# Moving an SBUF arena by 32 bytes against the activations that stand ahead of it

## What is computed

```python
h = rms_norm(x, attn_norm_g)
proj = h @ w_in                      # q, k, v of two branches, q of the third, 3 gates
m = rms_norm(mem, mem_norm_g)
mk, mv = split(m @ w_mem_kv)
y_a = neighbourhood_attention(qa, ka, va, na_rpb) @ w_branch_a
y_b = dilated_mixture(qb, kb, vb, t5_bias) @ w_branch_b
y_c = memory_attention(qc, mk, mv) @ w_branch_c
merged = gates[0] * y_a + gates[1] * y_b + gates[2] * y_c
x = x + merged @ w_out
h = rms_norm(x, ffn_norm_g)
# router: logits, top 4 of 32, softmax over the four
# expert e: gu = h @ w_gu[e] + b_gu[e]; a = (clip(u) + 1) * (g * sigmoid(1.702 g)); y = a @ w_dn[e] + b_dn[e]
x = x + weighted sum of the experts' y
out = rms_norm(x, final_norm_g)
```

## Time and profile before

| | us |
|---|---|
| median of 3 runs | 1217.89 (1217.21 to 1218.4) |
| the profiled execution, its own time | 1218.3 |
| its span, first to last instruction | 1216.5 |
| TensorE busy in it | 1166.8 |
| HBM read in it | 453.13 MB |

### The profile page before, as it was taken

One profiled execution on the slowest core, in us unless ns is written; L12 is line 12 of the kernel. 1 busy time (PEld: TensorE's weight loads), 2 busy tenths in 40 slices (PEclk: granted clock), 3 DMA queues, 4 the chain that ended last, 5 costly groups with the idle time before them and its releaser, 6 DMA issues.

```text
span 1216.5 us, 14185 instructions
## 1 busy us (share of the span) xinstructions
PE 1166.8 (96%) x6145; PEld 595.8 (49%) x6145; DVE 246.4 (20%) x511; ACT 269.7 (22%) x579; POOL 206.4 (17%) x89
## 2 busy tenths in 40 slices
PE   8999999999999999999999999998999999999996
PEld 7989877898433333333343333333333333333332
DVE  3145132233411121111111211111111111111112
ACT  6457577445210111001010100100000000010002
POOL 5864766785000000000000000000000000000000
PEclk9999999999999999999999999999999999999999
DMA  8775644677999999999999999999999999999994
GB/s 278 262 244 198 212 155 154 226 278 256 424 430 431 430 434 434 415 435 432 431 432 432 430 434 433 433 432 433 433 430 431 431 430 432 430 432 431 431 431 207
DMA packets 62136, 455.15 MB, mean 374 GB/s; under 512 B 5129, under 2 KB 33705, under 8 KB 43512
## 3 DMA queue, kind: packets, MB, share of 16 engines
q1 hardware_dynamic: 62072, 454.22, 90.3%
HBM read 453.13 MB, written 1.07 MB: 373 GB/s over the span
## 4 chain that ended last, share of the span: by engine, by line
PE 65%; DMA 30%; ACT 2%; DVE 1%; POOL 1%; issue 1%; DVEq 0%; SPq 0%; ACTq 0%; POOLq 0%
PE ps L591 63%; DMA arena<-in_expert_w_gate_up 27%; DMA arena<-in_expert_w_down 3%; PE ps L904 1%; PE ps L646 1%; PE ps L898 1%; POOL w_lowc L580 0%; DMA arena<-in_mem 0%; POOL w_lowa L580 0%; ACT arena L1106 0%; ACT arena L1096 0%; ACT L1120 0%; ACT w_high L1076 0%; DVE x_normed L1562 0%; PE ps L642 0%
## 5 line engine op out<-in xcount | busy, mean ns | idle before, releaser
L591 PE MATMUL ps<-arena,gathered_T 128*64 128x512 f32 x2034 | 472.8, 613 | 29.2 <-DMA arena<-in_expert_w_gate_up 29.2
L591 PE MATMUL ps<-arena 128*64 128x512 f32 (+6 forms) x1490 | 316.4, 562 | 3.4 <-issue 2.1
L591 PEld LDWEIGHTS ps<-arena,gathered_T 128*64 128x64 f32 x2034 | 144.9, 140 | 296.5 <-issue 269.2
L591 PEld LDWEIGHTS ps<-arena 128*64 128x64 f32 (+3 forms) x1490 | 113.3, 149 | 196.2 <-issue 193.6
L1229 ACT COPY arena<-ps 128x256 f32<-128x256 f32 x32 | 11.9, 372 | 350.5 <-PE ps L898 350.5
L1506 DVE TENSOR_SCALAR arena<-arena 128x128 f32<-128x128 f32 x64 | 19.3, 344 | 307.2 <-PE ps L898 307.2
L1512 DVE TENSOR_SCALAR arena<-ps 128x512 f32<-128x512 f32 x32 | 22.1, 692 | 275.6 <-PE ps L591 275.6
L1220 ACT ACTIVATE gathered_T<-ps,g_cols 128x128 f32<-128x128 f32 x128 | 36.6, 368 | 173.4 <-PE ps L591 173.4
L591 PEld LDWEIGHTS ps<-arena,x_normed 128*128 128x128 f32 x512 | 59.5, 191 | 24.8 <-issue 24.3
L591 PE MATMUL ps<-arena,x_normed 128*128 128x128 f32 x512 | 65.4, 281 | 0.2 <-DVE arena L1463 0.2
L1239 ACT COPY arena<-ps 128x512 f32<-128x512 f32 x31 | 18.2, 586 | 172.2 <-PE ps L591 172.2
(11 more groups left out here) (229 smaller groups left out, 897.5 us busy)
## 6 DMA issues: line engine op xcount, KB each, us to landing
arena<-in_expert_w_gate_up SPq DMA_DIRECT2D x53, 4096.0 KB, 37.9
arena<-in_expert_w_down SPq DMA_DIRECT2D x61, 2048.0 KB, 38.2
arena<-in_expert_w_gate_up SPq DMA_DIRECT2D x19, 2048.0 KB, 10.8
arena<-in_w_in SPq DMA_DIRECT2D x29, 1024.0 KB, 5.2
arena<-in_expert_w_down SPq DMA_DIRECT2D x6, 1024.0 KB, 38.6
arena<-in_expert_w_gate_up SPq DMA_DIRECT2D x4, 1024.0 KB, 7.1
arena<-in_w_out SPq DMA_DIRECT2D x4, 1024.0 KB, 5.8
arena<-in_w_mem_kv SPq DMA_DIRECT2D x3, 1024.0 KB, 11.5
```

The source lines that it names most:

```text
L591: return nc.tensor.matmul(out, lhsT, rhs, start=start, stop=stop, **kw)
```

## The change

The start of the arena is rounded up to a multiple of 64 as before, and 32 bytes are added: 38944 instead of 38912. Everything that counts from `base` moves with it: ring, weight parts, memory, attention and merged parts, all scratch. Everything made ahead of it stays. No instruction is added, removed or put elsewhere.

```diff
-        base = -(-nc.sbuf_base // 64) * 64
+        base = -(-nc.sbuf_base // 64) * 64 + 32
         MOE0 = RING * CHUNK
         arena = nc.alloc_sbuf_tensor_at("arena", [P, ARENA], F32, offset=base)
```

## The result

| | before | after |
|---|---|---|
| median of 6 runs each, us | 1217.55 (1215.71 to 1218.4) | 1223.88 (1222.14 to 1227.39) |
| ratio | | 1.0056, 95% interval 1.0043 to 1.0069 |
| profiled execution: its own time and its span, us | 1218.3, 1216.5 | 1222.51, 1220.7 |

The changed kernel is slower by 6.3 us by the medians (5.2 to 8.4 by the interval of the ratio, which is worked out from all runs and not from the two medians). The prediction was 1219.2 us with a range up to 1222.5: it fails, and so does its likeliest outcome, no difference that a measurement can tell.

The account below looks back on a forecast made before the run. TensorE bounds the front, before 300 us, and the DMA rate everything behind it. Front terms 1.90 + 0.57 + 0.2 - 1.30 = +1.37 us, taken as +1.3 on the median of 1217.89, gave 1219.2 us; range 1215.5 to 1222.5.

Parts of the forecast that it names:

- TensorE's sum: Front, ahead of 300 us: matmuls whose operands go from different to equal places add +1.37 us of TensorE time.
- A: Front: twelve narrow chunks with h_T_parts moving, 576 matmuls from 116.7 to 120.0 ns, +1.90 us.
- B: Front: seven narrow chunks with h_T_parts stationary, 336 matmuls from 118.3 to 120.0 ns, +0.57 us.
- C: Front: 64 matmuls with late_high moving and merged_T_parts stationary, priced like A, +0.2 us.
- D: Front: ten wide chunks, 240 matmuls from 232.1 to 226.7 ns, -1.30 us.
- The expert stream at no cost: Weight transfers from 304 to 1186 us: no cost taken, bounds 0 and 1.2% of 882 us, 10.6 us.
- the packets' case: Expert stream: packets 32 bytes past a multiple of 64 are slower, 1220.5 to 1229.8 us; chance 0.10.
- third rival: Expert stream: packets 32 past a multiple of 64 take longer into SBUF, up to 1229.8 us; chance 0.10.
- No effect: Front: the 3 and 5 ns differences come from something else, such as PSUM bank or neighbours; 1217.9 us; chance 0.12.
- The place itself: Front: each operand's own place sets matmul pace, not the relation; -5.1 us, 1212.8 us; chance 0.07.
- Expert matmuls, casts and vector work without a cost: Expert matmuls stay at 592 ns; ACT's casts and VectorE's scaling take the same time at either place; 0 us.
- ACT's squares: 1056 ns in the arena, 1105 ns from x_tokens to x_normed; taken as 0, upper bound +0.6 us.

Follow-up runs that it names:

- e2: Only the ring of weight slots 32 bytes higher than in the kernel before, scratch behind it kept at a multiple of 64: 1226.35 us, ratio 1.0070.
- e4: The changed kernel measured again, beside the kernel before: 1224.05 us, ratio 1.0052.
- f4: One chunk per weight transfer from expert 4 on, as in f3, with the arena 32 bytes higher: 1242.96 us, ratio 1.0206 to the kernel before.
- g1: Kernel before with the arena left in place and the activation tensors ahead of it moved down 32 bytes, to multiples of 256: 1218.84 us, ratio 1.0008.
- e3: Kernel before with only the scratch areas behind the ring 32 bytes higher, ring left in place: 1217.41 us, ratio 1.0000.
- f2: Kernel before with the arena 256 bytes higher and 64 floats shorter: 1217.53 us, ratio 0.9993.
- f3: Kernel before with one chunk per weight transfer from expert 4 on (packets of 8192 bytes), arena where it was: 1226.33 us, ratio 1.0068.
- e1: Kernel before with the arena 64 bytes higher and 16 floats shorter: 1223.06 us, ratio 1.0049.
- f1: Kernel before with the arena 128 bytes higher and 32 floats shorter: 1222.37 us, ratio 1.0039.
- g2: Kernel before with the activation tensors moved down to multiples of 256 and the arena 32 bytes higher: 1222.08 us, ratio 1.0037.
- h1: Kernel before with the arena 224 bytes higher and 56 floats shorter: 1221.86 us, ratio 1.0036.
- h2: f3's one-chunk transfers with the arena 224 bytes higher: 1240.52 us, ratio 1.0179 to the kernel before.

## Why the prediction was wrong

**What bounds the kernel: right.** Ahead of 300 us TensorE, behind it the DMA rate alone. It is by this that 0.59% of a rate became 5 us.

**TensorE's sum: right.** Forecast +1.37 us, and by the starts of the matmuls in the two traces: A, 62.85 us instead of 61.32 over eleven of the twelve chunks (the twelfth, in 6, waited for 1.3 us in the trace before), for twelve +1.7 (forecast +1.90); B, 39.92 instead of 39.40, +0.52 (+0.57); C, 7.36 instead of 7.23, +0.13 (+0.2); D, 53.28 instead of 54.39, -1.11 (-1.30). Together +1.2 us. A was over-priced a little because two of its chunks, in 2 and in 3, ran at 117.9 ns before and not at the 116.7 of in 9 that was taken for all. D was over-priced a little because two of its ten chunks, at 76 and 136 us, gained 1.3 to 1.7 ns a matmul and not 5; on the other side the window of the earlier trace rows for in 26 was cut a little short, since the starts of its matmuls stand 233.4 ns apart in the trace before and not 232.1. The whole front, from the first matmul of mem 1 to the last of out, scatters by a microsecond from one execution to the next; in the traces of the five kernels with equal places (the changed one, e2, e4, f4, g1) it took 276.5 to 278.0 us, on average 277.4, in the four with the places of before (before, e3, f2, f3) 275.1 to 276.5, on average 276.1: +1.3 us. TensorE's largest wait between 16 and 298 us went from 2.9 us to 3.4 us. By its letter that is one of the prediction's signs of being wrong, but it is the same wait for ACT and 0.5 us of it, so no new wait took the front's place:

```profile
PE ps L646 <- ACT arena L1106: 3.4, 3, 2.5
```

**The expert stream at no cost: the step that failed.** The prediction took the earlier trace rows, a transfer into x_tokens at 32, as evidence that such packets cost nothing, and gave the packets' case 0.10. The right mechanism was its third rival, but for the boundary, which is 256 bytes and not 64 (e1, f1 and f2), and its bound of 1.2%, 10.6 us, held the measured 0.59% and 5.2 us. Its sign, a stream below 429 GB/s, came by halves: 427 from 400 to 500 us, but 430 from 900 to 1000 us; the long stretch tells it clearly. Two things went wrong in this step.

First, the stretch was too short to show what was asked. 0.6% of 1.5 us is 9 ns, half a packet in eighty, as the text itself could have worked out from its own limit of 0.13%: no row of 1.5 us decides such a question, and the gap of one packet was taken as nothing.

Second, even exact times of its packets would not have shown it. In the changed kernel all packets into the ring start 32 past a multiple of 256, and yet the stretch from 292 to 293.5 us (all packets of 8192 bytes, into the arena) and the stretch of the earlier trace rows, 312.5 to 314 us, read

```profile
DMA packets 77, 0.63 MB, mean 421 GB/s; under 512 B 0, under 2 KB 0, under 8 KB 0
...
q1 hardware_dynamic: 77, 0.63, 99.1%
...
DMA packets 83, 0.64 MB, mean 429 GB/s; under 512 B 3, under 2 KB 3, under 8 KB 5
```

The first gives 0.991 x 16 x 1500 ns / 77 = 308.9 ns a packet, the time of an aligned one; the second 429 GB/s, more than the 426 of the earlier trace rows. In the busy stretch that begins at 300 us the single packets take the old time (309 ns for 8192 bytes) up to about 315 us and some 3 to 10 ns more from there on. The loads of the front behave alike: in one that keeps every DMA engine busy for some 64 packets, the first 50 or so are at the old time and the last ones at the longer one. How long a packet takes hangs on the packets around it too, and not on its own place alone. At the start of every kernel, x is loaded into x_tokens, in 128 packets of 8192 bytes. x_tokens stands 32 past a multiple of 256 in the kernel before and in the changed one alike, but the packets into the arena ahead of this load start at 0 in the one and 32 past in the other. From 9.5 to 10.5 us both move packets of this load alone, before and then after:

```profile
q1 hardware_dynamic: 48, 0.39, 92.9%
```
```profile
q1 hardware_dynamic: 50, 0.41, 98.3%
```

That is 309.7 and 314.6 ns a packet; of the 128, 5 took more than 310 ns before and all 128 after. It looks as if a lag builds up behind the engine that is hidden until it has grown; the runs show when the longer times begin, but that reading of them is only argued. The eight packets per engine that x_tokens takes are in any case fewer than those after which the price was seen here.

The Trainium skill (DMA: Bandwidth & Descriptors, section How a descriptor splits into AXI transactions) tells of the boundary of 256 bytes for reads, and the prediction set it aside as 0.9 to 1.7 us by its beats. The boundary agrees with the runs: 64 and 128 bytes past are slow (321.44 and 321.59 MB), 256 is free (322.95 MB). The beats don't: with 309 ns for 8192 bytes a beat of 32 bytes is 1.2 ns. By the Trainium skill's counting, an estimate, that would make 1.2 ns at 32 bytes, 4.8 at 128 and 8.4 at 224; the packets of 16 and 32 KB in the traces took 4.6 to 4.9, 3.6 to 3.8 and 4.6 to 4.9 ns more.

**The other rivals.** No effect: fell, as the paces moved to where the relation puts them (g1, with packets at 0). The place itself: fell with mem_T_parts' and merged_T_parts' unmoved paces and with g2. Expert matmuls, casts and vector work without a cost: right, by the row of line 591 above and by e3; in the changed kernel ACT's casts of the earlier trace rows still take 1046 to 1047 ns and VectorE's scaling of the earlier trace rows 750 and 752. ACT's squares of the earlier trace rows, the one row that spoke for a cost, still take 1056 ns in the arena now that it stands at 32, and 1105 ns from x_tokens in g2 where that stands at 0: it wasn't the place. Nor were the 276 ns of the transposes in the earlier trace rows, which is one long instruction in the mean; the median is 272 ns against both.

## What to carry to other kernels

In a stage where the DMA engines are full, the start of every destination in SBUF modulo 256 is part of the price: here 3.6 to 6 ns a packet, 0.5 to 0.6% with packets of 16 to 32 KB and 1.7% with packets of 8 KB. Align the base of a ring of buffers to 256 bytes and make its slots multiples of that; whoever adds a small tensor ahead of it should round the base again. And before a row is taken as evidence that something costs nothing, work out how much of the effect that would decide the case could be seen in it: a question of a thousandth wants a stretch of hundreds of microseconds, not eighty packets.

## What the runs showed of the hardware

- **Packets into SBUF that don't start on a multiple of 256 bytes take 3.6 to 6 ns longer** on average in a full stream, at 32, 64, 128 and 224 bytes past it, whether they carry 8, 16 or 32 KB; at 256 past they don't. The price doesn't grow with the distance (h1, h2). All these lengths are multiples of 256, so such a packet also ends off one: the runs don't tell whether the start or the end costs, nor why.
- **It isn't paid by the first packets of a busy stretch** (308.9 ns at 292 us in the changed kernel, 314.9 ns at 817 us in f4), and packets at one place pay it or not by the packets around them (the load of x, 309.7 and 314.6 ns).
- **The pace of an fp32r matmul of the front goes by the difference of the two operands' places modulo 256**, more finely than equal or different. Weights minus h_T_parts, and the pace in the chunks in 9 (h_T_parts moving) / in 22 (stationary) / in 26 (wide), in ns, by the starts of the matmuls:

| difference | kernels | in 9 | in 22 | in 26 |
|---|---|---|---|---|
| 0 | after, e2, e4, g1, f4 | 120.0 | 119.8 | 226.7 |
| 32 | e1, g2 | 118.4 | 116.7 | 233.2 |
| 96 | f1 | 118.6 | 119.9 | 233.5 |
| 192 | h1, h2 | 117.8 | 117.8 | 233.4 |
| 224 | before, e3, f2, f3 | 116.7 | 118.3 | 233.4 |

 Kernels of one difference agree to 0.1 ns, though the places themselves differ (e1 and g2, before and f2). The difference alone doesn't fix the pace: at 192 it is 113.3 ns in the second chunk with h_T_parts moving and 117.8 ns in 9, at 224 116.7 ns in 9 and 117.9 ns in 2 and in 3. What else it hangs on stays open. The Trainium skill (SBUF — State Buffer, section Who interferes with whom) gives TensorE two independent read ports; by that the table would have one row. Which difference is best was not tried further: the fronts of h1 and h2 took 275.7 us, 0.4 us less than the average of those with the places of before, and a kernel with that difference and aligned packets would gain less than these measurements can tell.
